# Two transformer layers on one core: the dense units' 512 columns walked from the last to the first

## The reference

```python
# first layer
h = rms_norm(x, norm1_g) * (1 + scale1) + shift1
qa, ka, va, qb, kb, vb, qi, ki, wi, gates = split(h @ w_in)
y_a = dsa_sparse_attention(qa, ka, va, qi, ki, wi)        # top-k chosen keys
y_b = differential_attention(qb, kb, vb, lam, subln_g)
merged = g_a * (y_a @ w_up_a) + g_b * (y_b @ w_up_b)
x = x + gate1 * (merged @ w_o)
x = x + gate2 * ((silu(h2 @ w_ff1) * (h2 @ w_ff3)) @ w_ff2)
# second layer
rq, rk, rv, rg, cq, ckv, krope, gr, gm = split(rms_norm(x) @ w_in_2)
a_ret = (rms_norm(retention(rq, rk, rv)) * silu(rg)) @ w_br
a_mla = causal_block_attention(q, k, v) @ w_bm            # q, k, v from cq, ckv
x = x + (sigmoid(gr) * a_ret + sigmoid(gm) * a_mla) @ w_o
x = x + square(relu(h2 @ w_up)) @ w_down
x = x + sigmoid(rms_norm(x) @ w_ple_gate) * (p @ w_ple)
```

## Time and profile before

| What | Value |
|---|---|
| median of three runs | 1978.51 us |
| the profiled execution's own time | 1980.14 us |
| its span, first to last instruction | 1978.3 us |
| PE busy | 1951.8 us, 99% |
| VectorE, ScalarE, GpSimd busy | 1066.4, 807.4, 117.9 us |
| share of the chain of waits on PE | 93% |
| share of that chain on line 776 | 47% |
| mean granted TensorE clock | 0.999 |

### The profile page before, as it was taken

The page is one execution under the profiler, slowest core; times in us unless marked ns, Lnnn a source line. Parts: engine busy times, 40 slices in busy tenths (PEclk is TensorE's granted clock), DMA queues, the critical chain, the costliest instruction groups (busy, mean ns, idle before and its releaser), DMA issues.

```text
span 1978.3 us, 24265 instructions
## 1 busy us (share of the span) xinstructions
PE 1951.8 (99%) x9224; PEld 1603.3 (81%) x9224; DVE 1066.4 (54%) x1695; ACT 807.4 (41%) x1358; POOL 117.9 (6%) x138
## 2 busy tenths in 40 slices
PE   7999999999999999999999999999999999999998
PEld 6778777888888888888888888878888888888887
DVE  6687877456443543475545454466653453434354
ACT  5343555634222233343232323587752342322343
POOL 3140000002000000200000000000000200000011
PEclk9999999999999999999999999999999999999999
DMA  9842212122323332322222222211223332323321
GB/s 373 322 173 86 65 47 104 61 88 71 105 87 89 114 92 78 114 85 85 85 86 85 85 85 74 65 56 45 65 87 106 130 104 86 107 89 101 97 94 64
DMA packets 196578, 199.64 MB, mean 101 GB/s; under 512 B 7547, under 2 KB 170448, under 8 KB 194064
## 3 DMA queue, kind: packets, MB, share of 16 engines
q1 hardware_dynamic: 192416, 175.15, 28.1%
q0 software_dynamic: 4080, 23.40, 3.0%
HBM read 194.33 MB, written 4.19 MB: 100 GB/s over the span
## 4 chain that ended last, share of the span: by engine, by line
PE 93%; DVE 3%; ACT 3%; issue 1%; DMA 1%; SPq 0%; DVEq 0%; ACTq 0%
PE bank L776 47%; PE bank L1283 4%; PE bank L1029 4%; PE bank L741 4%; PE bank L866 4%; PE bank L852 3%; PE bank L1543 3%; PE bank L1355 2%; PE bank L1084 2%; PE bank L1013 1%; PE bank L896 1%; PE bank L1261 1%; PE bank L979 1%; PE bank L1272 1%; PE bank L1303 1%; PE bank L1219 1%
## 5 line engine op out<-in xcount | busy, mean ns | idle before, releaser
L1659 ACT ACTIVATE w_hi<-raw 128x2048 fp32r<-128x2048 f32 (+4 forms) x164 | 283.3, 1728 | 399.8 <-PE bank L776 292.9
L2425 DVE TENSOR_TENSOR w_lo<-raw,w_hi 128x2048 fp32r<-128x2048 f32 (+4 forms) x163 | 336.8, 2067 | 147.6 <-ACT w_hi L1659 145.7
L776 PE MATMUL bank<-h_hi,w_hi 128*128 128x512 f32 x864 | 337.2, 390 | 0.0
L776 PE MATMUL bank<-h_hi,w_lo 128*128 128x512 f32 x864 | 336.1, 389 | 0.0
L776 PE MATMUL bank<-h_lo,w_hi 128*128 128x512 f32 x864 | 336.1, 389 | 0.0
L776 PEld LDWEIGHTS bank<-h_lo,w_hi 128*128 128x128 f32 x864 | 162.2, 188 | 34.1 <-issue 0.5
L776 PEld LDWEIGHTS bank<-h_hi,w_hi 128*128 128x128 f32 x864 | 162.2, 188 | 33.8 <-issue 0.5
L776 PEld LDWEIGHTS bank<-h_hi,w_lo 128*128 128x128 f32 x864 | 162.2, 188 | 33.6
L776 PE MATMUL bank<-u_hi,w_hi 128*128 128x512 f32 x256 | 99.6, 389 | 0.0
L776 PE MATMUL bank<-u_lo,w_hi 128*128 128x512 f32 x256 | 99.6, 389 | 0.0
L776 PE MATMUL bank<-u_hi,w_lo 128*128 128x512 f32 x256 | 99.6, 389 | 0.0
(11 more groups left out here) (581 smaller groups left out, 4148.5 us busy)
## 6 DMA issues: line engine op xcount, KB each, us to landing
raw<-in_w_in SPq DMA_DIRECT2D x49, 1024.0 KB
raw<-in_w_ff SPq DMA_DIRECT2D x44, 512.0 KB
raw<-in_w_up SPq DMA_DIRECT2D x16, 1024.0 KB
raw<-in_w_down SPq DMA_DIRECT2D x16, 1024.0 KB
raw<-in_w_o SPq DMA_DIRECT2D x8, 1024.0 KB
raw<-in_w_br SPq DMA_DIRECT2D x8, 1024.0 KB
raw<-in_w_in SPq DMA_DIRECT2D x13, 512.0 KB
raw<-in_w_ff SPq DMA_DIRECT2D x8, 768.0 KB
```

The source lines that it names most:

```text
L776: last = nc.tensor.matmul(dst, a, b, start=k == n == 0, stop=k == last_k and n == 2)
L1659: nc.scalar.activation(w_hi[:, slot, 0:width], raw[:, slot, 0:width], ACT.Copy).then_inc(hi_done, 1)
L2425: v.tensor_tensor(w_lo[:, slot, 0:width], raw[:, slot, 0:width], w_hi[:, slot, 0:width].bitcast(F32), ALU.subtract).then_inc(lo_done, 1)
```

## The change

Both the moving operand and the PSUM output of the one matmul statement in `tiles_by_k` are given with a step of minus one along the row. The first column that TensorE reads is column 511 of the slab, and the first that it writes is column 511 of the bank. Each column of the result is still the same sum, in the same place and in the same order of its terms. The stationary operand, the waits, the banks, the semaphores and the order of the instructions on every engine stand as they did; no instruction is added or taken away.

```diff
@@ -773,7 +773,7 @@
                     for dst, col in dsts:
                         a_hi, a_lo = w_tile(slot, k, row, col)
                         for n, (a, b) in enumerate(((a_hi, x_hi), (a_hi, x_lo), (a_lo, x_hi))):
-                            last = nc.tensor.matmul(dst, a, b, start=k == n == 0, stop=k == last_k and n == 2)
+                            last = nc.tensor.matmul(dst[:, ::-1], a, b[:, ::-1], start=k == n == 0, stop=k == last_k and n == 2)
                 last.then_inc(mm_done, 1)
```

## The result

The changed kernel takes 2005.78 us (median of four runs, 2005.75 to 2005.99), against 1978.51: 27.3 us more, a ratio of 1.0135 with a 95% interval of 1.0123 to 1.0147. It is slower, where no change was forecast.

What follows compares the result with a forecast made beforehand. TensorE (PE), busy 1951.8 of 1978.3 us, was taken as the bound. Read, write, fixed price and gain were each taken as 0, so the median stayed at 1978.5 us; range 1974 to 2865 us.

Steps and rivals of the forecast that it cites:

- the first of the four prices: Line 776's turned read of the moving operand: each column still costs one read, so 0; bounded above by 838 to 881 us.
- half pace: Rival on line 776: columns joined into one access only when ascending, 0.43 to 0.44 us a matmul, 2817 to 2860 us; 21%.
- the case that was forecast: No change: line 776's matmuls stay at 0.2267 us, 1978.5 us in all, own range 1974 to 1984 us; 62%.
- The second, the write: Line 776's turned write, adding into PSUM: taken to cost nothing, like the read, since it is turned together with it.
- the rule that was weighed: Skill text set against no cost on line 776: read strictly, a step of minus one is not contiguous and half pace holds.
- The third, a fixed price: A price for each line 776 matmul, such as restarting the operand's stream: at most 0.08 us each, 330 us; taken as 0.
- That rival: A small price for each line 776 matmul, 2 ns to 0.08 us: 8 to 330 us more, 1987 to 2309 us; 10%.
- a new address costs nothing there: Argument against a small price: line 776's three terms each read another tensor, yet all take 389 ns in steady rows.
- the fourth: A possible gain on line 776: at most 4128 x 0.013 = 54 us could vanish; no reason for it seen, taken as 0.
- The 0.013 us: Part of a line 776 matmul's 0.2267 us that is not columns, said to stand between any two matmuls as weights are exchanged.
- the slow path of plain float32: Rival on line 776: turned operand treated as plain float32, two records a matmul, 0.633 us more each, about 4590 us; 3%.
- The direction is not taken up: Rival: the engine walks line 776 upward as before, giving the forecast's time; no separate chance stated.

Runs made afterwards that it cites:

- mix_blocks: Kernel before, line 776 reading and writing blocks of columns last to first, width by stage: 233.3 ns a matmul for 8 to 32 columns, 226.7 for 64 and 128.
- e_write: Kernel before with only line 776's PSUM output walked downward, moving operand upward: 1979.98 us, ratio 1.0004.
- mix_lines: Kernel before, line 776's columns in pairs or fours, by stage: blocks last to first, upward within, 233.3 ns a matmul; blocks upward, down within, 226.7.
- e_shift16: Kernel before, all walks upward, line 776's weight tiles taken 16 columns (64 bytes) further on: 2005.87 us, ratio 1.0135.
- e_read: Kernel before with only line 776's moving operand walked downward, PSUM output upward: 2006.67 us, ratio 1.0144.
- mix_width: Kernel before, line 776 walked differently by stage; 256-column halves 118.3 ns downward, 120.0 upward; one downward term of three, 231.1 on average.

## Why the prediction was wrong

The step that failed is the first of the four prices, "the cost is 4128 x 0 = 0" for the turned read. It measured 6.67 ns a matmul, 27.5 us in all, and 0.2333 us stood where 0.2267 was forecast. The argument for nothing, that columns side by side upward are side by side downward too, looked at too small a neighbourhood: in mix_blocks even blocks of 32 columns taken backward pay in full. The stated range holds 2005.8 us only because it had to reach over half pace; the case that was forecast had 1974 to 1984. The second, the write, was right: e_write's ratio is 1.0004. On PSUM the rule that was weighed (the Trainium skill, "PSUM — Partial Sum Buffer", section "Specifications (TRN2)": any pattern that isn't contiguous slows matmuls) doesn't show here for a step of minus one: the price would have been in e_write. Nor do swapped pairs or fours cost anything in mix_lines, where each 8-byte line is still written whole.

The third, a fixed price, was put at nothing, with 2 to 80 ns kept as a rival. That rival's size held, 6.67 ns and 2005.8 us within its 1987 to 2309, but not its mechanism: a fixed price for each matmul would show at every width, and downward matmuls of 320 columns have the upward 13.3 ns beside their columns and those of 256 have 11.7. What was held against it, that "a new address costs nothing there", is true of the three terms (389 ns in each group; the earlier trace rows has one of them), but not of a new place relative to the weight load: e_shift16 pays in full.

The reasoning that misled is that of the fourth. The 0.013 us beside the columns were taken for a constant that "stands between any two matmuls here, whatever their columns". It is no constant: for 256 to 512 columns it was 11.7 to 34 ns in these runs, by the order in which the moving operand is read and by the place, width and step of the weight load. The trace of before had rows against it, which the prediction didn't read. The index stage has 24 upward matmuls with weight tiles of 68 columns, placed every 272 bytes (PE in order of time, kernel before; the last row is the next line's first):

```profile
96.94 0.39 PE L741 MATMUL bank<-h_hi,w_hi 128*68 128x512 f32 x1
...
102.49 0.41 PE L866 MATMUL bank<-w_hi,h_hi 128*128 128x512 f32 x1
```

5.55 us / 24 = 231.3 ns, 4.6 more than line 776's. Had it been read, the question would have been what 226.67 depends on, and the two answers open to it, the width and the place of the weights, both leave room for a price that the direction changes.

Line 776 itself has such rows, where nothing but time lies between dear matmuls and cheap ones. Behind a plain float32 matmul of the last stage it starts upward like this (kernel before):

```profile
1935.49 0.40 PE L776 MATMUL bank<-h_lo,w_hi 128*128 128x512 f32 x1
...
1937.35 0.39 PE L776 MATMUL bank<-h_hi,w_hi 128*128 128x512 f32 x1
...
1940.75 0.39 PE L776 MATMUL bank<-h_hi,w_hi 128*128 128x512 f32 x1
```

The first eight take 1.86 us, about 232 ns each, and the next fifteen 3.40 us, 226.7 each. So 226.67 is what a run of upward matmuls settles at in this layout, and not what each of them costs from the first on.

The rest went as argued. PE is the bound, and the 27.5 us came out on the end undiminished (27.3); PE's share of the chain is 93% as before; the groups of lines 866, 1283 and 1543, which were not edited, kept their means (390 to 403 ns on 866, 389 on the other two). Half pace and the slow path of plain float32 did not occur. "The direction is not taken up" is refuted by e_read.

Shown is this: the price is on the read of the moving operand; it depends on the order of reads over 256 bytes and not on the sign of the step; it appears in full without any downward step when the weights are set off against the moving operand, and goes when both are moved together by 32 to 128 bytes. That the two reads collide in the memory, and that an upward run falls into a step in which they do not, is a reading that fits most of this, not something a row shows. Why the downward walk of 512 columns finds no favourable place at any of the shifts tried, why 16 bytes are an exception, and why a smaller weight load does not help, stays open. No version here beats the kernel before.

## What to carry to other kernels

The time between two matmuls beyond their columns isn't a constant: here, for upward matmuls of 512 columns, it settles at 13.3 ns with the places that this kernel gives to weight tile and moving operand, and at 17 to 23 ns when one of them is moved alone by less than 256 bytes. On line 776, 20 ns in place of 13.3 are 1.35% of this kernel. So move both by the same amount (32 to 128 bytes were tried) or one by 256 bytes (64 columns, tried once), and look at the odd-shaped group of the trace and at the first matmuls behind a pause: their distances show what the regular ones owe to their layout. In these runs a downward or blockwise walk is free on the PSUM side, and on the read side as long as 64 float32 columns at a time go upward.

## What the runs showed of the hardware that was not expected

- Matmuls of 256 columns have 118.3 ns downward and 120.0 upward in long stretches (mix_width). That is not the direction alone: six upward ones in a short stretch of the kernel before take 0.71 us, 118 ns each (the last row is the next width's first):

```profile
885.36 0.28 PE L1229 MATMUL bank<-rq_hi,rk_hi 128*128 128x256 f32 x1
...
886.07 0.22 PE L1229 MATMUL bank<-rq_hi,rk_hi 128*128 128x128 f32 x1
```

- A single downward matmul among two upward ones raises the sum of the three by 13.3 ns, twice what each costs when all go down.
- Weight tiles with a step of 2 columns cost as much as any ill-placed tile (233.3 ns); with a step of 8 the turn of a 512-column matmul rises to 244 to 247 ns.
